# The start of a two-layer encoder kernel: x loaded first, shift and scale applied by halves of the channels, parameter rows loaded from ScalarE's queue

## What is computed

```
cond = jax.nn.silu(c)
for l in range(DEPTH):
    mod = cond @ w_mod[l] + b_mod[l]
    sh_m, sc_m, g_m, sh_f, sc_f, g_f = [m[:, None, :] for m in jnp.split(mod, 6, axis=-1)]
    h = rms_norm(x, pre_mix_g[l]) * (1.0 + sc_m) + sh_m
    z = h @ w_in[l]
    ...
```

## Time and profile before

| | us |
|---|---|
| three runs | 1463.50, 1463.55, 1457.72 |
| their median | 1463.5 |
| the profiled execution | 1458.68 |
| its span | 1457.1 |
| TensorE busy in the span | 1309.0 |
| VectorE busy | 938.3 |
| ScalarE busy | 709.3 |
| TensorE busy in the first 46.4 us | 11.99 |
| first product of `w_in` starts | 46.48 |

### The profile page before, as it was taken

The page is one execution under the profiler, slowest core; times in us unless marked ns, Lnnn a source line. Parts: engine busy times, 40 slices in busy tenths (PEclk is TensorE's granted clock), DMA queues, the critical chain, the costliest instruction groups (busy, mean ns, idle before and its releaser), DMA issues.

```text
span 1457.1 us, 16745 instructions
## 1 busy us (share of the span) xinstructions
PE 1309.0 (90%) x5901; PEld 1041.5 (71%) x5901; DVE 938.3 (64%) x1315; ACT 709.3 (49%) x1068; POOL 117.8 (8%) x158
## 2 busy tenths in 40 slices
PE   1897989799999999997988997899999999999990
PEld 1775447688888788876774474778887878788880
DVE  5956781665565457457476516686687668667885
ACT  4444441632122132136345514485687568657884
POOL 1370060000000000003300000200000000000002
PEclk9999999999999999998999998899999999999995
DMA  9931332146454464463542000797699679868995
GB/s 337 337 124 32 138 121 72 60 131 212 149 183 164 145 217 154 157 218 85 222 168 82 6 29 0 289 385 268 229 306 351 209 237 365 280 218 287 371 385 187
DMA packets 142632, 288.05 MB, mean 198 GB/s; under 512 B 6974, under 2 KB 48492, under 8 KB 142572
## 3 DMA queue, kind: packets, MB, share of 16 engines
q1 hardware_dynamic: 132172, 252.39, 49.9%
q0 software_dynamic: 10256, 34.87, 6.7%
q10 hardware_dynamic: 144, 0.00, 0.0%
HBM read 266.01 MB, written 21.23 MB: 197 GB/s over the span
## 4 chain that ended last, share of the span: by engine, by line
PE 78%; DVE 10%; ACT 5%; issue 4%; DMA 2%; ACTq 0%; POOL 0%; SPq 0%; DVEq 0%; POOLq 0%
PE ps L602 19%; PE ps L604 19%; PE ps L603 19%; PE ps L614 3%; PE ps L956 3%; PE ps L955 3%; DVE acc L1452 3%; PE ps L764 2%; PE ps L783 2%; PE ps L743 2%; ACT spl L1293 1%; PE ps L752 1%; DVE spl L1849 1%; DMA x<-in_x 1%; DMA mraw<-in_moe_w_down 1%
## 5 line engine op out<-in xcount | busy, mean ns | idle before, releaser
L1849 DVE TENSOR_TENSOR spl<-mraw,spl 128x1024 fp32r<-128x1024 f32 (+2 forms) x288 | 311.5, 1130 | 86.4 <-ACT spl L1293 85.5
L1293 ACT ACTIVATE spl<-mraw 128x1024 fp32r<-128x1024 f32 (+2 forms) x288 | 266.3, 979 | 118.1 <-PE ps L956 91.4
L1093 ACT ACTIVATE spl<-raw 128x2048 fp32r<-128x2048 f32 (+2 forms) x56 | 100.7, 1799 | 233.1 <-PE ps L604 194.9
L602 PE MATMUL ps<-hT,spl 128*128 128x512 f32 x416 | 164.7, 396 | 8.1 <-DVE hT L1513 8.1
L1436 DVE TENSOR_TENSOR spl<-raw,spl 128x2048 fp32r<-128x2048 f32 (+2 forms) x56 | 120.7, 2158 | 74.7 <-ACT spl L1093 74.1
L603 PE MATMUL ps<-hT,spl 128*128 128x512 f32 x416 | 163.4, 393 | 0.0
L604 PE MATMUL ps<-hT,spl 128*128 128x512 f32 x416 | 163.4, 393 | 0.0
L602 PE MATMUL ps<-spl,xgT 128*128 128x512 f32 (+1 forms) x384 | 147.1, 383 | 14.7 <-DVE spl L1849 11.8
L604 PE MATMUL ps<-spl,xgT 128*128 128x512 f32 (+1 forms) x384 | 144.4, 376 | 0.0
L603 PE MATMUL ps<-spl,xgT 128*128 128x512 f32 (+1 forms) x384 | 144.3, 376 | 0.0
L1452 DVE SCALAR_TENSOR_TENSOR acc<-raw,cond,acc 128x512 f32<-128x512 f32 x154 | 118.7, 771 | 5.4
(11 more groups left out here) (323 smaller groups left out, 2311.4 us busy)
## 6 DMA issues: line engine op xcount, KB each, us to landing
raw<-in_w_mod SPq DMA_DIRECT2D x48, 1024.0 KB, 6.0
mraw<-in_moe_w_down SPq DMA_DIRECT2D x40, 1024.0 KB, 7.8
mraw<-in_moe_w_gate SPq DMA_DIRECT2D x34, 1024.0 KB, 6.6
mraw<-in_moe_w_up SPq DMA_DIRECT2D x34, 1024.0 KB, 6.7
mraw<-in_moe_w_gate SPq DMA_DIRECT2D x16, 768.0 KB, 6.5
mraw<-in_moe_w_up SPq DMA_DIRECT2D x16, 768.0 KB, 7.8
raw<-in_ffn_w_gate SPq DMA_DIRECT2D x11, 1024.0 KB, 8.2
raw<-in_ffn_w_up SPq DMA_DIRECT2D x11, 1024.0 KB, 5.2
```

What stands on the lines that cost most here:

```text
L602: mm(o, lh, rh, start=start, stop=False)
L1093: A(spl[:, s % SPLS, 0, 0:n], raw[:, r % RAWS, 0:n], ACT.Copy).then_inc(hi_ready, 1)
L1293: A(spl[:, (SB + j) % SPLS, 0, c], mraw[:, j % MRAWS, c], ACT.Copy).then_inc(half_ready, 1)
L1849: ins = V.tensor_tensor(o[:, 1, c], mraw[:, j % MRAWS, c], o[:, 0, c].bitcast(F32), ALU.subtract)
```

## The change

It has six parts.

1. `plan()` puts column block 2 (the first half of the scale) second and block 1 (the second half of the shift) third, by `column_of`; the units of the third to fifth blocks stand between and behind the two first units of `w_in`.
2. x is loaded in four tiles with a semaphore each, ahead of all units on SyncE's queue.
3. `parameters()` moves to ScalarE's queue, behind the load of c and ahead of the wait for c.
4. ScalarE scales x, and TensorE turns chunks 0 to 3, ahead of the parameter rows. The turns go to banks 4 to 7.
5. Scale and shift are applied to chunks 0 to 3 once the first two column blocks are there, and the products of part 0, kh 0, start then; the other two column blocks and chunks 4 to 7 follow among these products (`in_proj_first`).
6. In this first `prenorm` ScalarE writes `full` for even chunks too; VectorE's instruction for them goes.

```diff
+def column_of(m):
+    return {1: 2, 2: 1}.get(m, m % MODC)
 def plan():
-    for m in range(4):
+    for m in range(2):
         mod(m)
     for l in range(L):
         for part in range(3):
             for kh in range(2):
                 units.append(("win", l, part, kh))
-                if l == 0 and part == 0 and kh == 1:
-                    mod(4)
+                if l == 0 and part == 0:
+                    for m in ((2, 3), (4,))[kh]:
+                        mod(m)
...
 sync
+            for t in range(T):
+                eng.dma_start(x[:, t, :], a["x"][0, P * t:P * t + P, :]).then_inc(x_dma[t], 16)
             for r, u in enumerate(UNITS):
...
-                if r == 1:
-                    eng.dma_start(x[:], a["x"][0].rearrange("(t p) d -> p t d", p=P)).then_inc(x_dma, 16)
-                if r == RAWS - 1:
-                    parameters()
 tensor
+            def turn_first(k):
+                for t in range(T):
+                    last = tr(ps[:, 4 + k % 4, P * t:P * t + P], xn[:, t, P * k:P * k + P])
+                last.then_inc(xT_ps, 1)
+
+            def in_proj_first():
+                u = unit_of(0, 4, 512)
+                eng.wait_ge(lo_ready, 1)
+
+                def product(t, kk):
+                    return mm3(ps[:, t, :], u(kk, P * t, P), hi_lo(hT, kk, 0, S), kk == 0, False)
+
+                for kk in range(4):
+                    eng.wait_ge(hT_ready, kk + 1)
+                    for t in (0, 1):
+                        product(t, kk)
+                mod(2, 7)
+                for k in range(4, 7):
+                    turn_first(k)
+                for kk in range(4):
+                    product(2, kk)
+                product(3, 0)
+                product(3, 1)
+                mod(3, 7)
+                product(3, 2)
+                product(3, 3).then_inc(w_used, 1)
+                eng.wait_ge(mod_out, 4)
+                turn_first(7)
...
             eng.wait_ge(const_ready, 1)
+            eng.wait_ge(xn_ready, T)
+            for k in range(4):
+                turn_first(k)
             eng.wait_ge(par_dma, 16 * 14)
             for i in range(2):
                 last = tr(ps[0:P, 0, P * i:P * i + P], prow[:, i, :])
             last.then_inc(col_ps, 1)
-            for m in range(3):
-                mod(m, 7)
...
+            mod(0, 3)
+            mod(1, 3)
 scalar
             eng.dma_start(cond[:, 0, :], a["c"][0].rearrange("(p k) -> p k", k=KD)).then_inc(c_dma, 16)
+            parameters()
             eng.wait_ge(c_dma, 16)
...
+            prenorm(0, range(1))
+            hi(0)
+            prenorm(0, range(1, 4))
...
+            hi(1)
+            prenorm(0, range(4, KD))
 vector
-            mod_sum(0)
+            mod_half(0, 0)
             eng.wait_ge(rms_ready, T)
             V.reciprocal(rinv[:], rms[:]).then_inc(xn_scale, 1)
+            mod_half(0, 1)
             mod_sum(1)
             eng.wait_ge(col_ready, 1)
-            mod_evict(0, 7)
+            mod_evict(0, 3)
+            mod_evict(1, 3)
+            prenorm(0, range(1))
+            lo(0)
+            prenorm(0, range(1, 4))
             mod_sum(2)
-            mod_evict(1, 7)
...
-            mod_sum(3)
+            mod_half(3, 0)
             mod_evict(2, 7)
-            lo(0)
+            mod_half(3, 1)
             mod_evict(3, 7)
+            lo(1)
+            prenorm(0, range(4, KD))
+            softplus()
```

More of the change, by code:

```diff
@@ L72, in mod @@
         for kh in range(2):
-            units.append(("mod", m // MODC, m % MODC, kh))
-    for m in range(4):
+            units.append(("mod", m // MODC, column_of(m), kh))
+    for m in range(2):
         mod(m)
@@ L680, in projections @@
             def projections(l):
-                for kh in range(2):
-                    in_proj(l, 0, kh)
+                if l:
+                    in_proj(l, 0, 0)
+                else:
+                    in_proj_first()
+                in_proj(l, 0, 1)
                 if l == 0:
@@ L1047, in _ @@
             last.then_inc(col_ps, 1)
-            for m in range(3):
-                mod(m, 7)
-            eng.wait_ge(col_ready, 1)
-            eng.wait_ge(xn_ready, T)
-            for k in range(KD):
-                if k == 7:
-                    mod(3, 7)
-                    eng.wait_ge(mod_out, 4)
-                for t in range(T):
-                    last = tr(ps[:, k, P * t:P * t + P], xn[:, t, P * k:P * k + P])
-                last.then_inc(xT_ps, 1)
+            mod(0, 3)
+            mod(1, 3)
             for l in range(L):
@@ L1117, in update, with prenorm @@
                 pre_stat(s + 1, T - 1)
[L1119 removed]
+            def prenorm(s, chunks=range(KD)):
                 c = modn if s >= 2 else modc
                 b = 2 * (s % 2)
[L1122 removed]
+                for q in chunks:
                     eng.wait_ge(xT_ps, KD * (s + 1) if s == 2 else KD * s + q + 1)
                     if q == 0:
[L1126 to L1128 removed]
+                        eng.wait_ge(mod_out, MODC * (s // 2) + (2, 10, 4)[s])
+                    if s == 0 and q == 4:
+                        eng.wait_ge(mod_out, 4)
+                    bank = 4 + q % 4 if s == 0 else q
+                    if q % 2 or s == 0:
                         if q > 1:
                             eng.wait_ge(hT_ready, KD * s + q - 1)
[L1131 removed]
+                        A(full[:, q % 2, :], ps[:, bank, :], ACT.Identity, scale=c[:, b + 1, q:q + 1],
                           bias=c[:, b, q:q + 1])
[L1133 removed]
+                    A(hT[:, 0, q, :], ps[:, bank, :], ACT.Identity, scale=c[:, b + 1, q:q + 1],
                       bias=c[:, b, q:q + 1]).then_inc(hT_hi, 1)
@@ L1385, in experts, with parameters @@
                         post_stat(3, t - 1, ym[:, t - 1, :], yg[:, t - 1, 0, :])
+            def parameters():
+                eng.wait_ge(prow_zero, 1)
+                rows = [a["b_mod"].rearrange("l (k p) -> (l k) p", p=P)]
+                rows += [a[n].rearrange("l (k p) -> (l k) p", p=P) for n in (
+                    "pre_mix_g", "pre_ffn_g", "q_norm_g", "kv_norm_g", "conv_b", "lru_ba", "lru_bx", "lru_lambda")]
+                rows += [a["conv_w"].rearrange("l w (j p) -> (l w j) p", p=P), a["sgu_b"].rearrange("l g p -> (l g) p")]
+                at_row = 0
+                for n, src in enumerate(rows):
+                    k = src.shape[0]
+                    dst = prow[0:k, 0, :] if n == 0 else prow[at_row:at_row + k, 1, :]
+                    at_row += k if n else 0
+                    eng.dma_start(dst, src).then_inc(par_dma, 16)
+                assert at_row == 78
+                for dst, src in (
+                        (cs[:], a["cs_table"]), (trig[:], a["trig_table"]),
+                        (router[:], a["moe_router"][0].rearrange("(k p) e -> p k e", p=P))):
+                    eng.dma_start(dst, src).then_inc(par_dma, 16)
             eng.dma_start(cond[:, 0, :], a["c"][0].rearrange("(p k) -> p k", k=KD)).then_inc(c_dma, 16)
+            parameters()
             eng.wait_ge(c_dma, 16)
@@ L1403, in _ @@
             A(sp[:, 2], sp[:, 1], ACT.Ln).then_inc(sp_c, 1)
-            for i in range(2):
-                hi(i)
+            hi(1)
+            prenorm(0, range(4, KD))
             for l in range(L):
-                prenorm(2 * l)
+                if l:
+                    prenorm(2 * l)
                 mixer(l)
```

59 lines of the change are left out of this document (18 added, 41 removed).

## The result

| | before | after |
|---|---|---|
| median of 7 runs each, us | 1461.63 | 1467.36 |
| lowest and highest | 1456.92, 1463.55 | 1466.91, 1469.96 |
| profiled execution, its span | 1458.68, 1457.1 | 1469.32, 1467.8 |
| first sum of VectorE starts | 6.80 | 12.57 |
| first product of `w_in` | 46.48 | 33.19 |

The ratio of the runs is 1.0050, interval 1.0034 to 1.0065: the change makes the kernel slower by 5 to 9.5 us, about 0.5%. The medians differ by 5.7 us. TensorE starts on `w_in` 13 us sooner and reaches the gates 5.5 us later. Executions of one kernel differ as well, and they do so with the granted clock: of 28 more executions of the kernel before, on another chip, those of 1461.3 to 1462.4 us had a clock of 0.961, those of 1467.4 to 1467.6 one of 0.956.

What follows compares the result with a forecast made beforehand. TensorE was taken as the bound, with time to be had at its start, held by a chain over three engines. Gates at 85.7, plus 1.7 for clock, 87.4 against 84.2, given as +3.3; 1463.5 + 3.3 = 1466.8 us, range 1457 to 1473.

Steps and rivals of the forecast that it cites:

- the prediction's own last line: Signs against the forecast: sguw copy ends before 76 us, silu later than 9, or `lo(2)` waits for its data.
- the third rival: Loads bunch up from 43.3 us, so part 1's units come late: adds 1 to 3 us, 1468 to 1470; chance 0.15.
- x and the column blocks: Loads at the start: x in at 9.4 us, VectorE's first sum at 14.0 (parameters cost up to 2.0), not 6.80.
- Parameter loads on ScalarE: At the start: 14 issues end at 7.1 us, silu at 8.7; x is scaled by 21.5, 6.4 us earlier.
- The rival that ScalarE gets stuck: ScalarE's parameter issues held by the load backlog, silu and squares late: gates 93.8, +9.6 us, 1473; chance 0.12.
- First product: TensorE's first product of `w_in` starts at 34.5 us, 12 us sooner than before.
- The second half: Last column blocks and chunks 4 to 7: VectorE waits 1.5 us or more for `mod(3)`; chunks end at 59.6.
- Where the two meet: VectorE needs 20.6 us from `softplus` to the sguw copy, at 80.2; TensorE ends part 0 at 68.5.
- Hidden edits: GpSimd's loads go 9 us later, after three column blocks, taken at 0; the load for `mod(3)` lands near 42.
- The third tile: In part 1, TensorE stands there at 76.1 us and waits 4.1 us for VectorE's copy of sguw.
- Clock: Behind the 4.1 us pause, half clock costs 1.7 us more (bounds 0 and 2.9), gates at 87.4.
- the early start carried through: Third tile doesn't wait if VectorE's chain is 4 us shorter; part 0 ends 2.6 us sooner; 1458.5 to 1461; chance 0.23.

Runs made afterwards that it cites:

- e6: The changed kernel with the 14 parameter loads back on SyncE's queue behind the first four column block units; ratio 1.0032 to the kernel before.
- e2: The changed kernel with VectorE's eviction of the fifth column block and its copy of sguw moved ahead of the convolution; ratio 1.0002 to the kernel before.
- e8: e7 with 16 unused turns of the identity matrix in TensorE's pause ahead of the spatial mix; ratio 0.9975 to the kernel before.
- e7: e2 with GpSimd's three loads of gains let go after two column blocks instead of three; ratio 0.9984 to the kernel before.
- e5: The kernel before with the copy of sguw and the fifth column block's eviction ahead of the convolution; ratio 0.9986 to the kernel before.
- e9: e8 with the parameter loads back on SyncE's queue behind four units; ratio 0.9972 to the kernel before.
- e10: The kernel before with only the 16 unused turns ahead of the spatial mix added, in both layers; ratio 0.9995 to the kernel before.

## Why the prediction was right, and where it was not

**The forecast, +3.3 us and within the bound of 0.5%, was right in sign and within the range** (1466.8 against 1467.36), though the ratio, with its interval up to 1.0065, stands right at that bound. The kernel before came out at 1461.6 over seven runs, not 1463.5, so the measured difference is 5.7 us by the medians and 7.3 by the ratio: about double the sum. That the time was met within 0.6 us is therefore luck: the base was too high by 1.9 us and the difference too small by 2.4. (The sum has a slip as well: 87.4 less 84.2 is 3.2.) By the prediction's own last line the forecast is wrong if `lo(2)` waits for its data, and it did, for 4.86 us. What the forecast named came about, the wait before the third tile and the half clock behind it, and so did the third rival, which the sum took at nothing. In the terms of the sum, up to the gates: part 0 was over at 65.8, 2.7 us sooner than forecast; then came a pause of 3.95 us and 1.8 us of half clock that the sum did not have; the pause before the third tile was 1.1 us shorter, the clock behind it cost the 1.7 us that were put in, and `mod(4)` and the turns took 0.3 us more. That gives 89.6 instead of 87.4.

- *x and the column blocks.* Right: first sum at 12.57, between the ends 12.0 and 14.0, nearer the early one. The parameters' transfers cost 1.0 us there (e6), not 2.0. That the loads of several issuers interleave is thus borne out (12.57 us with the parameters on ScalarE's queue, 11.60 with them behind the units), at half the price I took.
- *Parameter loads on ScalarE.* Right: 14 issues until 7.3 against 7.1, silu from 8.64. The rival that ScalarE gets stuck fell. That they cost nothing further on was wrong: without them the scaling of x starts 1.2 us sooner and `softplus` 2.1 (e6).
- *First product.* 33.19 against 34.5: two `mod` took 1.35 and 1.02, where I used 1.84. In e2 and e8 the second one did take 1.84, and there the first product came at 34.51 and 34.76.
- *The second half.* The mechanism was right, with all its waits: VectorE waits for `mod(3)` (1.2 us), TensorE for the chunks. The size was off: `softplus` at 56.71, where I had 59.6. Of these 2.9 us, 1.4 were there since the first product and the sums behind it. Most of the rest is TensorE's way to `mod(3)`: I charged it with 1.8 and 2.1 us for `mod(2)` and 12 turns, which took 1.05 and 1.51, and so it was there as soon as the sum was. For the same reason part 0 was over at 65.8, where I had 68.5.
- *Where the two meet.* Here the step failed that said VectorE has the same work as before from `softplus` to the copy, 20.6 us. It took 25.7, since `lo(2)` waited 4.86 us for data. "Hidden edits" took this at 0 and sent it to the third rival, which I gave 0.15 and 1 to 3 us. I had counted the load right (landing at 66.4 forecast, 67.7 found), but set it against a VectorE that was too late by 3 us and so hardly needed it. e2 and e7 show the two halves: with the copy early the gates come 3.8 us sooner, and with most of the wait for the unit gone as well, 9.3.
- *The third tile.* Right in kind: a pause of 2.98 us where 4.1 were forecast. Both ends came later, the copy at 82.4 instead of 80.2, and TensorE, held back by the pause before part 1 and the half clock behind it, at 79.5 instead of 76.1. e2 shows that it is this wait: with the copy early it is gone. e5 shows that the kernel before had slack there.
- *Clock.* Right for the one pause that the sum had: 0.51 behind it, and 1.8 us. The other pause cost as much again. Beyond the gates the view was too short: the profiled execution lost another 4.5 us by the dense part, with 10 us more at half clock, which no term of mine had.

The other rivals: the early start carried through only once the copy and the loads had been moved (e7, e9), which the change doesn't do.

## What to carry to other kernels

When two engines run in parallel with a few us between them, find the next place where the leader waits for the other, and do the sum there: a start that is 13 us earlier is worth nothing if the engine behind it has the same amount of work and gets its data later. Look for small instructions that others wait for behind large ones that nobody waits for yet; moving one copy of 0.68 us ahead of a convolution took back 3.8 of the 5.5 us at the gates, and the kernel was level with the one before. And a load that is released by a counter moves with that counter: list these loads, and set them against the holes in the transfers. Before a difference of a few us in the whole time is put down to an edit, compare how long each execution was at half clock behind it.

## What the runs showed of the hardware

- A unit of 1 MB landed in 5.0 to 5.2 us when little else was under way (three units of the change, issued between 33 and 42 us), and in 13.9 to 19.4 us beside GpSimd's loads of 3.7 MB (five units, before and after).
- 14 DMA issues on ScalarE's queue took 0.24 to 0.64 us each while four of SyncE's took 5.5 us together. The issues of one engine were not held by the backlog of the other.
- TensorE's pauses of 2.85, 2.98, 3.83 and 3.95 us were followed by a granted clock of half (1.2 of 2.4 GHz), and 16 idle turns in such a pause kept it full (e8, e10). In e9 half clock came behind the mix in spite of them (0.50 from 107 to 109 us); TensorE stood idle for some 2 us behind the turns there as in e8, so what makes the difference stays open.
- Behind the copy of `v` the profiled executions of thirteen kernels differ by up to 3.3 us and 7.1 us in two parts of the span, and by 6.8 and 13.9 us in the time at half clock there. No kernel falls out of this order.
